# Even units of the first expert product as one 512-column stream, with the halves added on GpSimd

## The reference, cut to what matters

```python
def peer(h, w_query, sub_keys, expert_u, expert_v):
    ...
    q = (hf @ w_query).reshape(T, PEER_HEADS, 2, PEER_HALF)
    scores = jnp.einsum("thpd,hpnd->thpn", q, sub_keys)
    ...                                    # top 16 of 128 keys twice, top 16 of the pairs
    gates = jax.nn.softmax(best_v, axis=-1)
    def body(xc):
        u = jnp.take(expert_u, xc["idx"], axis=0)
        vv = jnp.take(expert_v, xc["idx"], axis=0)
        a = jax.nn.gelu(jnp.einsum("td,thkd->thk", xc["h"], u))
        return jnp.einsum("thk,thkd->td", xc["g"] * a, vv)
```

## Time and profile before

| | |
|---|---|
| runs of the kernel | 2735.05, 2735.56, 2737.14 us (median 2735.56) |
| profiled execution | 2734.07 us, its span 2732.4 us |
| granted clock of TensorE | 0.998 of full speed over the span |
| first half of the expert product, layer 0 | from 977.8 to 1160.4 us of the span |
| first half of the expert product, layer 1 | about 1971 to 2154 us |

### The profile page before, as it was taken

One profiled execution on the slowest core, in us unless ns is written; L12 is line 12 of the kernel. 1 busy time (PEld: TensorE's weight loads), 2 busy tenths in 40 slices (PEclk: granted clock), 3 DMA queues, 4 the chain that ended last, 5 costly groups with the idle time before them and its releaser, 6 DMA issues.

```text
span 2732.4 us, 51120 instructions
## 1 busy us (share of the span) xinstructions
PE 2673.6 (98%) x18740; PEld 2410.4 (88%) x18740; DVE 2155.3 (79%) x3979; ACT 1425.0 (52%) x2240; POOL 131.8 (5%) x202
## 2 busy tenths in 40 slices
PE   6999989999999999999999999999999999999999
PEld 6999988899999999988888888899999988888887
DVE  6888884788876769888889887666589888898665
ACT  4555654455545555555544455555555555444454
POOL 0113130001010000000000010000000000000000
PEclk9999999999999999999999999999999999999999
DMA  8985462489775555555555688554555555555554
GB/s 323 316 309 194 154 212 72 142 290 308 261 279 184 198 180 186 181 172 174 166 176 174 211 290 289 192 163 162 167 187 186 177 169 171 171 172 176 186 195 150
DMA packets 157513, 550.84 MB, mean 202 GB/s; under 512 B 23280, under 2 KB 23792, under 8 KB 157040
## 3 DMA queue, kind: packets, MB, share of 16 engines
q1 hardware_dynamic: 131136, 464.64, 50.8%
q0 software_dynamic: 22176, 80.75, 8.8%
q10 hardware_dynamic: 3984, 2.45, 0.3%
HBM read 546.33 MB, written 1.44 MB: 200 GB/s over the span
## 4 chain that ended last, share of the span: by engine, by line
PE 72%; PEld 14%; DVE 6%; DMA 3%; issue 2%; ACT 1%; PEldq 0%; SPq 0%; ACTq 0%; DVEq 0%
PE acc L2682 17%; PE acc L2058 8%; PE acc L2689 8%; PE st L2045 6%; PE st L2049 6%; PE st L2046 6%; PE st L2058 5%; PE acc L2062 4%; PEld st L2058 3%; PE st L2062 3%; PE st L2649 2%; DVE w_lo L1046 2%; PEld st L2062 2%; DMA ring<-weights 2%; PEld acc L2045 2%
## 5 line engine op out<-in xcount | busy, mean ns | idle before, releaser
L1046 DVE TENSOR_TENSOR w_lo<-ring,w_hi 128x1024 fp32r<-128x1024 f32 x860 | 1056.0, 1230 | 384.8 <-ACT w_hi L536 164.8
L536 ACT ACTIVATE w_hi<-ring 128x1024 fp32r<-128x1024 f32 x860 | 901.1, 1052 | 293.8 <-DMA ring<-weights 208.5
L2045 PE MATMUL st<-h_both,w_hi 128*128 128x256 f32 x1680 | 415.7, 285 | 1.6 <-ACT arena L947 1.3
L2046 PE MATMUL st<-h_both,w_hi 128*128 128x256 f32 x1680 | 412.2, 283 | 0.0
L2045 PEld LDWEIGHTS st<-h_both,w_hi 128*128 128x128 f32 x1680 | 322.0, 192 | 9.7 <-issue 4.9
L2046 PEld LDWEIGHTS st<-h_both,w_hi 128*128 128x128 f32 x1680 | 322.2, 192 | 0.1
L2682 PE MATMUL acc<-w_hi,act_hi 128*128 128x512 f32 x1016 | 319.1, 395 | 0.4 <-ACT w_hi L536 0.4
L2682 PE MATMUL acc<-w_hi,act_lo 128*128 128x512 f32 x1016 | 313.0, 389 | 0.0
L988 ACT ACTIVATE act_hi<-arena 128x256 fp32r<-128x256 f32 x256 | 106.8, 418 | 373.4 <-PE acc L2689 369.1
L2058 PE MATMUL st<-h_both,w_hi 128*128 128x512 f32 x1184 | 297.2, 393 | 0.6 <-ACT w_hi L536 0.6
L2689 PE MATMUL acc<-w_lo,act_hi 128*128 128x512 f32 x1016 | 271.5, 389 | 0.0
(11 more groups left out here) (375 smaller groups left out, 3729.9 us busy)
## 6 DMA issues: line engine op xcount, KB each, us to landing
ring<-weights SPq DMA_DIRECT2D x864, 512.0 KB, 3.4
arena<-ada_weights POOLq DMA_DIRECT2D x104, 512.0 KB, 6.2
extra<-ada_weights POOLq DMA_DIRECT2D x48, 512.0 KB, 4.7
arena<-ada_weights SPq DMA_DIRECT2D x16, 512.0 KB, 13.3
arena<-const ACTq DMA_DIRECT2D x1, 1280.0 KB, 7.8
x_t<-params SPq DMA_DIRECT2D x1, 1024.0 KB, 11.3
extra<-crows POOLq DMA_DIRECT2D x2, 512.0 KB, 6.1
out<-arena SPq DMA_DIRECT2D x4, 256.0 KB, 2.1
```

The source lines that it names most:

```text
L536: nc_a.activation(w_hi[:, u % 3, :], ring[:, u % RING, :], ACT.Copy).then_inc(hi_ready, 1)
L1046: v.tensor_tensor(w_lo[:, u % 2, :], ring[:, u % RING, :], w_hi[:, u % 3, :], ALU.subtract)\
L2045: mm(dst(t), w, hi_t(t), start=start, stop=False, skip_group_check=True)
L2046: mm(dst(t), w, lo_t(t), start=False, stop=False, skip_group_check=True)
```

## The change

The 30 even units below 60 (`JOINED`) of each layer become wide. ScalarE copies the whole bank, 512 columns, to one of two buffers in `extra` (`even_pair`) and signals `u_even`. GpSimd adds the two halves into `experts[:, n, :]` and signals `joined`. The gelu of an even unit waits for `joined` and reads SBUF. TensorE takes the bank again at `u_even`.

```diff
+        JOINED = [n for n in range(HALF - 4) if n % 2 == 0]
+        def even_pair(n):
+            return ar(2 * T * (n // 2 % 2), 2 * T, base=extra)
...
                     if n in FOLDED:
                         src = dst
                         eng.wait_ge(sem("folded"), fold_count(l, n) + 1)
+                    if n in JOINED:
+                        src = dst
+                        eng.wait_ge(sem("joined"), join_count(l, n) + 1)
                     nc_a.activation(dst, src, ACT.Gelu_apprx_tanh).then_inc(sem("gelu"), 1)
...
                     if n in FOLDED:
                         nc_a.activation(experts[:, n, :], u_place(n)[:, T:2 * T], ACT.Copy).then_inc(sem("u_other"), 1)
+                    if n in JOINED:
+                        nc_a.activation(even_pair(n), u_place(n), ACT.Copy).then_inc(sem("u_even"), 1)
...
                 if l == 0:
                     ada_loads(8 * Q_WQ + ADA_RING, 8 * Q_LATE)
+                for n in JOINED:
+                    eng.wait_ge(sem("u_even"), join_count(l, n) + 1)
+                    two = even_pair(n)
+                    g.tensor_tensor(experts[:, n, :], two[:, 0:T], two[:, T:2 * T], ALU.add)\
+                        .then_inc(sem("joined"), 1)
                 if l == 0:
...
                         if m in FOLDED:
                             eng.wait_ge(sem("folded"), fold_count(l, m) + 1)
+                        elif m in JOINED:
+                            eng.wait_ge(sem("u_even"), join_count(l, m) + 1)
                         else:
                             eng.wait_ge(sem("gelu"), n_key + m + 1)
...
-                    if n in FOLDED:
+                    if n in FOLDED or n in JOINED:
                         wide(u_place(n), base + n)
```

More of the change, by code:

```diff
@@ L417, in build, with join_count @@
         FOLDED = [n for n in range(NKEYS) if (n < HALF - 4 and n % 2 == 1) or n >= HALF]
+        JOINED = [n for n in range(HALF - 4) if n % 2 == 0]
+        def even_pair(n):
+            return ar(2 * T * (n // 2 % 2), 2 * T, base=extra)
+        def join_count(l, n):
+            return len(JOINED) * l + sum(j < n for j in JOINED)
         def fold_count(l, n):
```

## The result

The change made the kernel slower: 2741.1 us, median of 20 runs (2739.26 to 2743.96), against 2736.04 us for the kernel before (20 runs on the same chips), a ratio of 1.0021 with a 95% interval of 1.0015 to 1.0027 (here and below the ratio is not the quotient of the two medians, and differs from it by up to 0.0005). That is 5 to 6 us. The forecast was 3.4 us more, 2739.0 on a scale where before stood at 2735.56.

A forecast was written before the change was run, and what follows sets the result against it. TensorE sets the pace, but over the last 13 units VectorE decides when unit 62 begins. Savings of -4.3 us plus +7.7 us for blocked adds gave +3.4 us, 2739.0 us; range 2731.6 to 2743.0.

The forecast's parts named there:

- within 0.2%: Outcome class for the whole kernel: a time less than 0.2% (5.5 us) from no change; chance 0.75.
- slower: Outcome class for the whole kernel: slower by over 0.2%, above 2741.0 us; chance 0.21.
- forecast band: Whole kernel: 2736.2 to 2741.1 us, for a price of 0.35 to 0.7 us per blocked add; chance 0.55.
- the dear price: Rival, units 46 to 58: each blocked add costs VectorE its whole length, 0.7 us or more; +5.9 us, 2741.5; chance 0.15.
- the late rhythm: Rival, even units before 46: VectorE, once late, stays late as its subtraction waits behind the add; +6.1 us, 2741.7; chance 0.10.
- TensorE's saving: Even units 0 to 46: each goes from 2.88 to 2.79 us, 0.09 saved, 2.16 us a layer, 4.3 in all.
- VectorE's full stretch: From the subtraction behind unit 46 to the fold of unit 59, VectorE has no spare time; 39.3 us before, about 43 predicted.
- the six later savings: Even units 48 to 58: what TensorE saves there is swallowed by its wait in front of unit 62.
- No price for the adds of units 0 to 44: Early even units: the add runs behind VectorE's w_lo subtraction and meets only one-input searches, so costs VectorE nothing.
- Price of a blocked add: Units 46 and 48 to 58: seven adds a layer cost VectorE 0.55 us each, 3.85 us a layer, 7.7 in all.
- The wait before unit 62: TensorE's wait for a ScalarE gelu, 0.94 us before, to grow to 2 us and more or move to w_lo.
- its rule: Trainium skill: a two-SBUF-input VectorE instruction and a GpSimd SBUF read block each other fully; 0.72 us an add, +5.8 us.

## Why the prediction was right, and where its sizes were off

The time fell inside the range and, by the measured 5 to 6 us, on the edge between "within 0.2%" and "slower". The mechanism was the one written down; the sum was short by about 2 us, by two terms that partly offset each other. In part it was luck: 2741.1 us is the upper edge of the forecast band, the range above it was there for the dear price and the late rhythm, neither of which came, and what took the time there was a term that the sum did not have.

- **TensorE's saving, 2.16 us a layer up to unit 46.** Measured 0.087 us a unit, 2.1 us with unit 46 itself. Right.
- **VectorE's full stretch decides when unit 62 begins, by the end of the fold plus 3.93 us.** Right to the hundredth: 3.93 again. That the six later savings are lost is right as well.
- **No price for the adds of units 0 to 44, ScalarE and GpSimd at nothing.** Right, shown by the run with these adds alone and by the one that only writes.
- **Price of a blocked add, 0.55 us.** Most single rows show 0.54, nearly the one I had chosen; but two of the seven in each layer met VectorE at a better moment (0.45 and 0.32 in layer 0, 0.51 and 0.44 in layer 1), and the stretch grew by 3.3 us and not 3.85. Mis-sized by 0.5 us a layer, the cautious way; of this 0.2 to 0.3 us is no matter of the adds, as the stretch itself grew shorter by that with wide units.
- **The wait before unit 62, "grown to 2 us and more".** It grew to 3.19, but I gave it no price beyond its length. This is the term that was missing: behind it TensorE runs at 1.2 GHz for a while, 1.48 us a layer. With the right sizes the sum is 2 x (-2.1 + 3.3 + 1.5) = +5.4 us. No wait that long stood in the stretch, but the trace of the kernel before had the price elsewhere. A narrow unit at 409.12 us, behind a wait of 2.50 us (and one of 2.98 a unit earlier), has the low clock and takes until 413.48, 4.36 us for 2.88: the same 1.48 us.

```profile
409.12 0.19 PEld L2045 LDWEIGHTS acc<-h_both,w_hi 128*128 128x128 f32 x1 [2.50 <-ACT w_hi L536]
...
412.36 1.19 PEld L2049 LDWEIGHTS acc<-h_both,w_lo 128*128 128x128 f32 x8
413.48 0.19 PEld L2045 LDWEIGHTS acc<-h_both,w_hi 128*128 128x128 f32 x1
```

```profile
409.30:412.70 3.40, 3.40 (x17) 3.40 (x18) 3.19 (x8) 2.25 (x3) 0.00 (x0) 0.50 0.57 193
```

- **The late rhythm.** It did not come about. VectorE's two-input sum at unit 32 was lengthened to 0.97 us, its subtraction behind unit 32 began 1.95 us behind the unit's end, that behind unit 34 0.99, and that behind unit 35 was back at 0.39.
- **The dear price and its rule.** Each add stops VectorE, but for 0.54 us at most in the change, and 0.58 in its repetition and in the version with units 46 to 58, less than the add's 0.72. The row that spoke for the dear price was read too dearly: the scale-and-add of 1.15 us was set against the fold's 0.42, but the same operation alone takes 0.47 us at least, so that it lost 0.67 and not 0.73.
- **What the profile would show.** The adds in the free rhythm are listed with 1.22 us and not 0.7, since their own wait for SBUF counts in; the 0.7 us are only the second part. In the full stretch they have 0.74 to 1.84. The rest, 43 us, waits for w_lo, a longer wait before unit 62, is there.

## What to carry to other kernels

An engine with little work is not a free place for it if it shares a path with the engine that is short of time: here seven adds on an idle GpSimd cost VectorE 3.3 us where doing them itself cost about 2. Ask of each moved operation where in the schedule the lender has spare time; 23 of the 30 adds were free, and the change was a gain if it stopped there. And look at what the delay passes through: 3 us of table loads that nobody needed yet turned VectorE's lateness into TensorE's, and moving them was worth more in the change (3.1 us a layer, half of it the clock) than choosing the right engine after it (1.1 to 1.4).

## What the runs showed of the hardware that was not expected

A wait has a tail on TensorE, though not in every execution. In the ten layer passes with a longest wait of 0.8 to 1.45 us, in front of unit 62 or 63, the clock stayed at 1.00. In the eight with an empty wait of 3.2 us it fell to 0.5 in seven. In five of them it fell 0.6 to 1.3 us after unit 62 had begun, so it is seen in the rows of the unit behind the wait and not in the wait itself, and units 62 and 63 lost 1.5 us. In the other two (layer 1 of the version with units 46 to 58 and of the one with folds on VectorE) it fell 0.6 and 1.1 us before unit 62 began, and they lost 2.7 and 2.5 us. The eighth, layer 0 of the version with folds, kept the full clock with the same wait.

What tells it from the others stays open, but it need not be anything in the kernel. Ahead of unit 0, where no version was edited, all 14 profiled executions have the same two waits of TensorE, 2.2 us near 490 and 2.1 us near 743. Behind the first the clock fell in 4 of the 14, behind the second in 3. Here are the 3.4 us from 0.4 us behind the end of the second on, in the kernel before (wait over at 740.78) and in the change (744.21):

```profile
741.20:744.60 3.40, 3.33 (x27) 3.08 (x26) 3.07 (x8) 2.01 (x5) 0.07 (x1) 1.00 0.97 357
744.60:748.00 3.40, 3.40 (x18) 3.40 (x18) 2.83 (x8) 1.81 (x4) 0.11 (x1) 0.50 1.00 387
```

A GpSimd operation that only waits for its turn at SBUF is listed as busy: the same add has 0.74, 1.22, 1.50 or 1.84 us in one profile.
